# Scan groups of a two-block model on one core: order of the copies out of PSUM, of the z projections and of one convolution tap

## Chip, cores and metric

One core of a Trainium2 chip runs the whole program. The metric is the device time of one execution in microseconds (us), as the median of several runs. The engines are TensorE (PE in the rows, its weight loads PEld), VectorE (DVE), ScalarE (ACT), GpSimd (POOL) and SyncE (SP). Times inside the profile count from the start of the span.

## What is computed

The reference is one transformer block (stick-breaking and differential attention, gated FFN) and after it one hybrid block, everything in fp32. The change lies in the scan branch and the conformer branch of the second block, over 528 tokens (16 meta tokens and 512):

```
u = rms_norm(h, w_norm_mix);  proj = u @ w_in      # conf_a, conf_g, z, xbc, dt, gates
c = conf_a * sigmoid(conf_g)
c = depthwise_conv(c, 31 taps) ...                  # conformer branch
xbc = silu(depthwise_conv(xbc, 7 taps) + b)         # x (2048), B (4 x 128), C (4 x 128)
y = forward scan + backward scan of (x, dt, B, C) + d_skip * x
y = rms_norm(y * silu(z), w_ssm_norm)
merged = gates1 * (c @ w_conf_out) + gates2 * (y @ w_ssm_out)
h = h + merged @ w_out;  h = h + expert_choice_ffn(rms_norm(h))   # 16 experts
```

The scans are done in chunks of 128 tokens: within a chunk by a masked product of C and B with decays, between chunks by states.

## The kernel before

Each engine has its own program, a list in a fixed order, and the engines meet by semaphores. All activations lie in SBUF with channels on the 128 partitions and the 528 tokens along the free dimension. Projections of the second block (`dense`, line 499, called by `proj`, 774) are 32 matmuls each: 8 blocks of the contraction by two halves of 264 columns and two weight reads. A projection fills a pair of PSUM banks; the pairs 0-1 and 2-3 alternate, and `open_` waits until the pair's last content was freed. Banks 4 to 7 serve the scan. `fill` counts a bank as filled, `free` as freed, `got` and `freed` are the waits for these.

The four **scan groups** (`for g in range(GROUPS)`, in the program of each engine) have eight heads each, and each group runs through three stages.

**Conv stage.** Six projections `xbc(g, i, j)`, tiles t = 0 to 5 (four of x, one of B at t = 2, one of C at t = 5). ScalarE copies each from PSUM to `XP`, two buffers (`conv_tile`, line 1316). VectorE runs the seven taps into `CO`, two buffers (line 1870 for the first, 1873 for the other six), with two conformer taps between them. ScalarE applies silu (`conv_silu`, lines 1387 and 1389). TensorE turns the tile into token-major form by five transposes into banks 4 and 5 (`turn`, line 836), and ScalarE copies them out (`take_turned`, lines 1399 and 1400). TensorE's order is projection t, then transpose t-2. ScalarE's order for step t is tile copy t, silu t-1, copy of the turned tile t-3.

**z stage.** GpSimd scales the turned x by decay weights (`scaled`, line 2142), TensorE multiplies them with B into a state in bank 6 (line 866), VectorE folds it into the backward snapshots `SNAP` (lines 1885 to 1890) and then runs eight conformer taps (`some_taps(8, ...)`). There are four such state products per group, and behind each TensorE has one projection of z, on which ScalarE applies silu (line 1422). Ahead of the stage ScalarE issues four DMAs that fetch decay sums for two chunks, spread over all partitions (`fr_load`, line 1364), into two buffers `FR`; GpSimd masks them (`masked`, line 2153) and ScalarE makes exponentials of them (`decays`, line 1375).

**Chunk stage.** For each of five chunks (the last has 16 tokens) TensorE has one projection (a gate or, in groups 0 to 2, one half of a conformer pair, or the next group's first tile), the transpose of the last chunk's output (`turn_y`, line 845, bank 5), the products with the snapshots and the state (885, 890), eight small ones for the diagonal part (895), the next state (901) and the product of B and C for the next chunk (905). VectorE adds the two tables (1899), multiplies them by B·C (1903), combines the outputs (1915 to 1932), updates the state (1939 to 1944), and multiplies the turned output into z (`gate_y`, 1815). It runs two and two conformer taps in between. Table transfers for chunk c+2 wait until chunk c's tables were used. The last transpose of a group, `turn_y(g, NC-1)` at line 907, stands behind the fifth chunk, and VectorE's `gate_y(g, NC-1)` too.

**Conformer products.** For each of eight tiles u TensorE projects `ca` (a) and then `cg` (gate). ScalarE writes sigmoid of `cg` to `SGB` (`conf_gate`, line 1323), VectorE multiplies it with `ca` out of PSUM into `CP` (three buffers; `conf_in`, line 1844), and that frees the bank pair of `ca`. Tiles 0 and 1 are projected before the first group, the others in the chunk stages of groups 0 to 2. The 31 taps of each of the eight tiles, 248 in all (`conf_taps`, lines 1830 and 1833), are worked off in a fixed order `TAP_ORDER`; `some_taps` takes the next ones, but none of a tile that is not yet there.

Weights come through a ring of four slots, one load per SP instruction in a fixed order; a load waits for the last reader of its slot. Gates that fit nowhere later are projected at places listed in `GATES_AT` (in group 3 one more, "late", behind the conv stage), copied out by ScalarE and stored to HBM by a DMA of its queue (`gates_out`, line 1333).

Behind the scan groups come the layer norm and the output projections (from line 925), routing, and the expert stage (line 1047 and about it).

## Time and profile before

| | |
|---|---|
| runs | 2829.73 us median of 3 (2828.01 to 2834.2) |
| profiled execution | 2834.3 us, its span 2832.5 us |
| busy, share of the span | PE 94%, PEld 57%, DVE 36%, ACT 23%, POOL 8% |
| mean granted clock | 0.97 |
| chain that ended last | PE 88%, DVE 6%, ACT 2%, issue 2%, DMA 1%, POOL 1% |
| costliest lines | L1047 (experts) 509.8 and 504.8 us, L504 (projections) 545.1 us for 2304 matmuls |

How to read it: busy shares are of the whole span, which has stages with quite different limits. "Idle before, releaser" gives how long an engine stood before an instruction and what ended this. The granted clock is the share of full speed that TensorE had; it has two levels, 0.50 (1.2 GHz) and 1.00 (2.4 GHz). The first projection of the second block starts at 743.67 us, group 0 at 807.30, and the last instruction of group 3 ends at about 1460 us.

### The profile page before, as it was taken

Reading aid. Unit: us, or ns where it says so; the run is one execution under the profiler, and the core shown is the slowest. Engines: PE = TensorE matmul, PEld = TensorE weight load, DVE = VectorE, ACT = ScalarE, POOL = GpSimd, SP = SyncE. Lnnn points to the kernel's source line nnn. Section 1 sums busy time; section 2 is a strip of 40 time slices with the busy share of each in tenths; the row PEclk is TensorE's granted clock in tenths of the full one; section 3 lists DMA queues with packets and bytes.
Section 4 is the critical chain, followed back from the end, with each engine's and each line's share of the span. In section 5 each row is a group of like instructions: output and inputs, shape, how many; then the busy total and the mean of one; then the engine's idle time right before and its main releaser. Section 6 shows DMA issues by size and latency. Waiting matters only on the chain.

```text
span 2832.5 us, 39942 instructions
## 1 busy us (share of the span) xinstructions
PE 2657.5 (94%) x17315; PEld 1616.0 (57%) x17315; DVE 1028.0 (36%) x1482; ACT 654.7 (23%) x1166; POOL 214.1 (8%) x218
## 2 busy tenths in 40 slices
PE   8998999999979989898979997999999999999996
PEld 6754478888757767676767996333333333333332
DVE  4335344433246776676765434111111111111111
ACT  3245432222122314131226223000000000001001
POOL 0022000000002112030120000000000000000000
PEclk9999999999989999999989999999999999999998
DMA  5200032222214123230431244999999999999993
GB/s 198 88 2 1 30 119 90 89 82 86 105 43 130 55 71 103 71 103 23 118 117 60 90 172 161 403 391 402 400 393 402 395 407 398 395 402 392 392 399 142
DMA packets 92618, 560.77 MB, mean 198 GB/s; under 512 B 15236, under 2 KB 48004, under 8 KB 59812
## 3 DMA queue, kind: packets, MB, share of 16 engines
q1 hardware_dynamic: 40320, 514.89, 46.1%
q10 hardware_dynamic: 47236, 30.42, 4.0%
q0 software_dynamic: 4896, 12.98, 1.7%
q8 instruction: 137, 2.24, 0.3%
q14 instruction: 29, 0.24, 0.0%
HBM read 541.97 MB, written 16.29 MB: 197 GB/s over the span
## 4 chain that ended last, share of the span: by engine, by line
PE 88%; DVE 6%; ACT 2%; issue 2%; DMA 1%; POOL 1%; ACTq 0%; POOLq 0%; DVEq 0%
PE PS L1047 35%; PE PS L504 17%; PE PS L949 4%; PE PS L727 4%; PE PS L723 4%; PE PS L724 4%; PE PS L954 2%; PE PS L698 2%; PE PS L631 2%; PE PS L582 1%; PE PS L578 1%; PE PS L579 1%; PE PS L517 1%; PE PS L1037 1%; DVE H L1833 1%
## 5 line engine op out<-in xcount | busy, mean ns | idle before, releaser
L504 PE MATMUL PS<-U,ring 128*128 128x264 f32 x2304 | 545.1, 397 | 18.7 <-DVE arena L1844 18.7
L1047 PE MATMUL PS<-expert_ring_low,U 128*32 128x512 f32 x4608 | 509.8, 594 | 0.9 <-DVE U L2058 0.9
L504 PEld LDWEIGHTS PS<-U,ring 128*128 128x128 f32 x2304 | 448.8, 197 | 107.6 <-issue 29.5
L1047 PE MATMUL PS<-expert_ring_high,U 128*32 128x512 f32 x4608 | 504.8, 592 | 0.0
L1047 PEld LDWEIGHTS PS<-expert_ring_high,U 128*32 128x32 f32 x4608 | 148.0, 110 | 336.9 <-issue 335.9
L1047 PEld LDWEIGHTS PS<-expert_ring_low,U 128*32 128x32 f32 x4608 | 146.2, 110 | 332.9 <-issue 331.9
L1833 DVE SCALAR_TENSOR_TENSOR H<-arena,par,H 128x528 f32<-128x528 f32 x240 | 190.7, 840 | 1.4
L2070 DVE TENSOR_TENSOR H<-H,PS 128x512 f32<-128x512 f32 x32 | 22.0, 688 | 438.6 <-PE PS L1047 423.2
L723 PE MATMUL PS<-UX,WF 128*128 128x512 f32 x352 | 137.9, 392 | 0.8 <-DVE UX L1593 0.8
L724 PE MATMUL PS<-UX,WF 128*128 128x512 f32 x352 | 137.0, 389 | 0.0
L1270 ACT ACTIVATE WF<-ring 128x1024 fp32r<-128x1024 f32 (+1 forms) x76 | 72.0, 948 | 245.8 <-PE PS L727 245.5
L1539 ACT ACTIVATE H<-PS 128x512 f32<-128x512 f32 x32 | 19.1, 597 | 457.9 <-PE PS L1047 457.9
L1718 DVE TENSOR_TENSOR WF<-ring,WF 128x1024 fp32r<-128x1024 f32 (+1 forms) x76 | 82.5, 1085 | 93.3 <-ACT WF L1270 93.2
L1873 DVE SCALAR_TENSOR_TENSOR SQ<-arena,par,SQ 128x528 f32<-128x528 f32 x144 | 110.4, 767 | 3.4
L2200 POOL DMA_INDIRECT residual_rows<-H,scatter_rows x16 | 25.1, 1572 | 931.4 <-DVE H L2084 931.4
L1375 ACT ACTIVATE ring<-ring,arena 128x128 f32<-128x128 f32 (+1 forms) x320 | 89.2, 368 | 19.1 <-POOL ring L2153 16.8
L727 PE MATMUL PS<-UX,WF 128*128 128x512 f32 x352 | 87.0, 389 | 0.0
L2076 DVE COPY U<-PS 128x256 f32<-128x256 f32 x32 | 13.6, 425 | 191.1 <-PE PS L1041 191.1
L1550 ACT ACTIVATE SQ<-PS 2x512 f32<-2x512 f32 x32 | 18.9, 591 | 260.6 <-PE PS L1047 260.2
L1959 DVE TENSOR_TENSOR RINGL<-ring,WH 128x1024 fp32r<-128x1024 f32 x32 | 38.9, 1224 | 102.1 <-ACT WH L1461 102.1
L723 PEld LDWEIGHTS PS<-UX,WF 128*128 128x128 f32 x352 | 66.1, 188 | 15.3 <-DVE UX L1593 1.2
L724 PEld LDWEIGHTS PS<-UX,WF 128*128 128x128 f32 x352 | 66.1, 188 | 14.1 <-issue 0.5
(326 smaller groups left out, 3195.4 us busy)
## 6 DMA issues: line engine op xcount, KB each, us to landing
expert_ring_low<-w_experts SPq DMA_DIRECT2D x96, 2048.0 KB, 11.7
expert_ring_high<-w_experts SPq DMA_DIRECT2D x96, 2048.0 KB, 11.3
ring<-w_gu SPq DMA_DIRECT2D x11, 2048.0 KB, 7.8
ring<-ssd_sums ACTq DMA_DIRECT2D x32, 512.0 KB, 7.8
ring<-w_xbc SPq DMA_DIRECT2D x8, 1536.0 KB, 6.6
ring<-w_down SPq DMA_DIRECT2D x8, 1408.0 KB, 6.0
ring<-w_in SPq DMA_DIRECT2D x5, 2048.0 KB, 7.9
ring<-w_conf SPq DMA_DIRECT2D x8, 1024.0 KB, 5.4
```

The lines of the kernel that those rows point to most:

```text
L504: last = nc.tensor.matmul(PS[0:M, banks[i], 0:hi - lo], lhs(k), rhs(k)[:, lo:hi], start=(k == 0), stop=(k == K - 1))
L631: last = nc.tensor.matmul(PS[:, 3 + o // 512, o % 512:o % 512 + SEQ - k2 * P], lower if k2 == kb else ones, SP(h)[:, ZO[k2]:ZO[k2] + SEQ - ...
L723: nc.tensor.matmul(PS[:, bank, :], hi[:, k, :], src[:, 0, k0 + k, :], start=(start and k == 0), stop=False)
L724: nc.tensor.matmul(PS[:, bank, :], hi[:, k, :], src[:, 1, k0 + k, :], start=False, stop=False)
L727: last = nc.tensor.matmul(PS[:, bank, :], lo[:, k, :], src[:, 0, k0 + k, :], start=False, stop=(stop and k == n - 1))
L949: nc.tensor.matmul(PS[:, banks[i], 0:HT], wh[:, k, :], x(k)[:, lo:hi], start=(first and k == 0 and x is high), stop=False)
L1047: mm = nc.tensor.matmul(PS[QUAD * t:QUAD * t + QUAD, bank, :], stat(t), move(t), start=start, stop=stop)
L1270: A(split(0, p), raw(p), ACT.Copy).then_inc(S("fw_high"), 1)
L1375: ins = A(FR[i % 2][d][0:n, h, 0:n], FR[i % 2][d][0:n, h, 0:n], ACT.Exp, bias=FT[0:n, c, j:j + 1])
L1718: V_.tensor_tensor(split(1, p), raw(p), split(0, p).bitcast(F32), SUB).then_inc(S("fw_low"), 1)
L1833: ins = V_.scalar_tensor_tensor(acc, CP[:, u % 3, j:j + T2], par[:, w0 + j:w0 + j + 1], acc, MUL, ADD)
L1873: ins = V_.scalar_tensor_tensor(co, xp[:, k:k + T2], par[:, w0 + k:w0 + k + 1], co, MUL, ADD)
```

## The change

- `take_turned(g, t-3)` comes first in ScalarE's step t, ahead of the tile copy.
- A new `mid_tap` on ScalarE computes the middle one of the seven taps straight from PSUM into `CO`, as a Copy with a per-channel scale, and frees the bank pair; it waits until `CO` was read for tile i-2. VectorE does the other six taps, each adding to `CO`.
- `conf_gate` on ScalarE also copies `ca` from PSUM into `CP` and frees the pair; VectorE's `conf_in` multiplies it by `SGB` in place, counted by a new semaphore `conf_input`.
- Two z projections of a group go ahead of the state products: one ahead of transpose 4, one behind it. The other two follow state products 0 and 1. State product 3 follows the projection of chunk 0.
- `fr_load(g, 0)` and `fr_load(g, 1)` go ahead of `take_turned(g, 3)` on ScalarE.
- The last output transpose and product of a group go behind the next group's second projection and first conv tile.
- Four memsets of pads are chained instead of counted.

```diff
@@ TensorE
+            def z_gate(g, s):
+                name = ("z", g, s // 2)
+                arrived(name)
+                proj(("zt", 4 * g + s), slot(name), slice((s % 2) * P, (s % 2) * P + P), name)
+
+            def back_state(g, s):
+                c = NC - 1 - s
+                n = CHUNKS[c][1]
+                pe.wait_ge(S("xwb_ready"), 4 * g + s + 1)
+                open_(("sb", g, c), 6)
+                fill(nc.tensor.matmul(PS[:, 6, :], BT[0:n, c, :], XW[0:n, s % 2, :], start=True, stop=True), ("sb", g, c))
...
                     if t >= 2 or (g > 0 and t == 1):
                         xbc(g, i, j)
+                    if g > 0 and t == 1:
+                        turn_y(g - 1, NC - 1)
                     if t >= 2:
                         turn(g, t - 2)
                 gates((g, "conv"))
+                z_gate(g, 0)
                 turn(g, 4)
+                z_gate(g, 1)
                 gates((g, "late"))
...
-                for s, c in enumerate(range(NC - 1, 0, -1)):
-                    t0, n = CHUNKS[c]
-                    pe.wait_ge(S("xwb_ready"), 4 * g + s + 1)
-                    open_(("sb", g, c), 6)
-                    fill(nc.tensor.matmul(PS[:, 6, :], BT[0:n, c, :], XW[0:n, s % 2, :], start=True, stop=True),
-                         ("sb", g, c))
-                    name = ("z", g, s // 2)
-                    arrived(name)
-                    proj(("zt", 4 * g + s), slot(name), slice((s % 2) * P, (s % 2) * P + P), name)
+                for s in range(3):
+                    back_state(g, s)
+                    if s < 2:
+                        z_gate(g, s + 2)
                 for c, (t0, n) in enumerate(CHUNKS):
...
                     gates((g, c))
+                    if c == 0:
+                        back_state(g, 3)
...
-                turn_y(g, NC - 1)
+            turn_y(GROUPS - 1, NC - 1)
@@ ScalarE
                 b = bank(("xb", g, t))
-                free(A(tok(XP[:, i % 2, 3:3 + T2], T2), PS[:, b:b + 2, 0:HT], ACT.Copy), ("xb", g, t))
+                A(tok(XP[:, i % 2, 3:3 + T2], T2), PS[:, b:b + 2, 0:HT], ACT.Copy)
+
+            def mid_tap(g, t):
+                i = 6 * g + t
+                b = bank(("xb", g, t))
+                if i >= 2:
+                    g2, t2 = divmod(i - 2, 6)
+                    if t2 in (2, 5):
+                        act.wait_ge(S("conv_ready"), i - 1)
+                    else:
+                        got(act, ("tr", g2, t2))
+                w = pcol("ssm_w", conv_row(g, t) * SSM_TAPS + MID_TAP)
+                free(A(tok(CO[:, i % 2, :], T2), PS[:, b:b + 2, 0:HT], ACT.Copy, scale=w), ("xb", g, t))
 
             def conf_gate(u):
                 got(act, ("cg", u))
                 if u >= 1:
-                    act.wait_ge(*freed(("ca", u - 1)))
+                    act.wait_ge(S("conf_input"), u)
                 b = bank(("cg", u))
                 free(A(tok(SGB[:, :], T2), PS[:, b:b + 2, 0:HT], ACT.Sigmoid), ("cg", u))
+                if u >= 3:
+                    act.wait_ge(S("conf_tap"), TAPS_TO[u - 3])
+                b = bank(("ca", u))
+                free(A(tok(CP[:, u % 3, 15:15 + T2], T2), PS[:, b:b + 2, 0:HT], ACT.Copy), ("ca", u))
...
                 for t in range(6):
+                    if t >= 3:
+                        take_turned(g, t - 3)
                     if g > 0 or t >= 2:
                         conv_tile(g, t)
+                        mid_tap(g, t)
                     if t >= 1:
                         conv_silu(g, t - 1)
-                    if t >= 3:
-                        take_turned(g, t - 3)
+                fr_load(g, 0)
+                fr_load(g, 1)
                 take_turned(g, 3)
                 gates_out((g, "conv"))
                 conv_silu(g, 5)
+                take_gate(g, 0)
                 take_turned(g, 4)
+                take_gate(g, 1)
                 gates_out((g, "late"))
-                fr_load(g, 0)
-                fr_load(g, 1)
...
+                take_gate(g, 2)
+                take_gate(g, 3)
                 decays(g, 0)
                 decays(g, 1)
@@ VectorE
             def conf_in(u):
-                got(dve, ("ca", u))
-                dve.wait_ge(*freed(("cg", u)))
-                b = bank(("ca", u))
                 if u >= 3:
                     conf_taps(TAPS_TO[u - 3])
-                    dve.wait_ge(S("conf_tap"), TAPS_TO[u - 3])
-                free(V_.tensor_tensor(tok(CP[:, u % 3, 15:15 + T2], T2), tok(SGB[:, :], T2), PS[:, b:b + 2, 0:HT], MUL),
-                     ("ca", u))
+                dve.wait_ge(*freed(("ca", u)))
+                dve.wait_ge(*freed(("cg", u)))
+                cp = CP[:, u % 3, 15:15 + T2]
+                V_.tensor_tensor(cp, SGB[:, :], cp, MUL).then_inc(S("conf_input"), 1)
...
-                    for k in range(SSM_TAPS):
-                        if k == 0:
-                            ins = V_.tensor_scalar(co, xp[:, 0:T2], par[:, w0:w0 + 1], None, MUL)
...
+                    side_taps = [k for k in range(SSM_TAPS) if k != MID_TAP]
+                    for n, k in enumerate(side_taps):
+                        if n > 0:
+                            dve.wait_ge(S("conv_tap"), (len(side_taps) - 1) * i + n)
+                        V_.scalar_tensor_tensor(co, xp[:, k:k + T2], par[:, w0 + k:w0 + k + 1], co, MUL, ADD)\
+                            .then_inc(S("conv_tap" if n < len(side_taps) - 1 else "conv_done"), 1)
                         if k in (2, 5):
                             some_taps(1, 2 * g + 2)
+                    if g > 0 and t == 0:
+                        gate_y(g - 1, NC - 1)
...
-                gate_y(g, NC - 1)
+            gate_y(GROUPS - 1, NC - 1)
```

Not shown: the new helper `take_gate(g, s)` holds what stood in the loop over s (wait for projection s of z, silu into `YT`), `conv_row` and `MID_TAP` are names for what was written out, and `mid_tap(0, 0)` and `mid_tap(0, 1)` stand behind the first two tile copies. VectorE's wait for `CO` moved into `mid_tap`.

## Rows read from the trace of the kernel before

**Rows 1.** Stretch: us; length; busy (instructions) of PE, PEld, DVE, ACT, POOL; clock; DMA; GB/s
```profile
1800.00:2000.00 200.00, 200.00 (x1852) 64.15 (x1848) 22.71 (x43) 16.61 (x28) 11.79 (x9) 1.00 1.00 400
```

**Rows 2.** TensorE's waits over the run: for whom; us in total, times, longest
```profile
PE PS L836 <- ACT arena L1400: 29.5, 12, 5.3
PE PS L504 <- DVE arena L1844: 18.7, 8, 8.0
PE PS L845 <- DVE arena L1932: 10.7, 5, 2.5
PE PS L866 <- POOL arena L2142: 10.5, 3, 3.5
```

**Rows 3.** ScalarE in order of time, one tile of group 1: start, us, engine, line
```profile
1003.98 0.61 ACT L1316 ACTIVATE arena<-PS 128x528 f32<-128x528 f32 x1 [8.04 <-PE PS L504]
1004.49 0.73 ACT L1389 ACTIVATE SQ<-SQ,par 128x528 f32<-128x528 f32 x1
...
1005.74 0.27 ACT L1400 ACTIVATE arena<-PS 16x128 f32<-16x128 f32 x1
```

**Rows 4.** TensorE in order of time, with the idle time before each
```profile
788.58 17.12 PE L504 MATMUL PS<-U,ring 128*128 128x264 f32 x64 [8.00 <-DVE arena L1844]
...
827.65 1.30 PE L836 MATMUL PS<-consts_sb,SQ 128*128 128x128 f32 x5 [5.32 <-ACT arena L1400]
828.74 8.64 PE L504 MATMUL PS<-U,ring 128*128 128x264 f32 x32
...
968.19 0.57 PE L845 MATMUL PS<-consts_sb,arena 16*128 16x16 f32 x4 [2.42 <-DVE arena L1932]
...
1006.15 0.74 PE L836 MATMUL PS<-consts_sb,arena 128*128 128x128 f32 x5 [2.20 <-ACT arena L1400]
```

**Rows 5.** TensorE: two projections at full rate, one at the last slow place
```profile
897.29 14.41 PE L504 MATMUL PS<-U,ring 128*128 128x264 f32 x64
...
1325.99 8.97 PE L504 MATMUL PS<-U,ring 128*128 128x264 f32 x32
```

**Rows 6.** Stretches of TensorE alone: us; length; busy; clock; DMA; GB/s
```profile
963.00:968.00 5.00, 2.77 (x24) 1.00 0.00 0
968.00:974.00 6.00, 5.81 (x16) 0.50 0.00 0
```

**Rows 7.** VectorE: first and last instruction of one conv tile, group 1
```profile
986.90 0.49 DVE L1870 TENSOR_SCALAR SQ<-arena,par 128x528 f32<-128x528 f32 x1 [0.69 <-ACT arena L1316]
...
992.57 0.76 DVE L1873 SCALAR_TENSOR_TENSOR SQ<-arena,par,SQ 128x528 f32<-128x528 f32 x1
```

**Rows 8.** ScalarE's queue: the four table transfers of group 1
```profile
1026.46 6.77 ACTq L1364 DMA_DIRECT2D ring<-ssd_sums  x4
```

**Rows 9.** VectorE in group 3: last snapshot, eight taps, tables of chunk 0
```profile
1392.27 0.68 DVE L1887 TENSOR_TENSOR arena<-arena 128x512 f32<-128x512 f32 x1
...
1393.71 5.52 DVE L1833 SCALAR_TENSOR_TENSOR H<-arena,par,H 128x528 f32<-128x528 f32 x8
1401.83 1.23 DVE L1899 TENSOR_TENSOR ring<-ring 128x1024 f32<-128x1024 f32 x1 [2.60 <-ACT ring L1375]
```

**Rows 10.** TensorE in group 3, chunks 0 and 1
```profile
1402.24 1.02 PE L885 MATMUL PS<-arena 128*128 128x512 f32 x2
1404.37 2.00 PE L895 MATMUL PS<-arena 128*128 128x64 f32 x16 [1.11 <-DVE arena L1903]
...
1422.10 2.04 PE L901 MATMUL PS<-arena 128*128 128x512 f32 x2 [3.58 <-DVE arena L1917]
...
1424.36 7.80 PE L504 MATMUL PS<-U,ring 128*128 128x264 f32 x32
```

**Rows 11.** ScalarE's queue and GpSimd in group 3: tables of chunk 2
```profile
1407.37 1.47 ACTq L1364 DMA_DIRECT2D ring<-ssd_sums  x2
...
1416.77 2.62 POOL L2153 TENSOR_SCALAR_AFFINE_SELECT ring<-ring 128x1024 f32<-128x1024 f32 x2 [27.70 <-DMA ring<-ssd_sums]
1419.36 1.04 POOL L2142 TENSOR_TENSOR arena<-arena,par 128x512 f32<-128x512 f32 x1
```

More of the change, by code:

```diff
@@ L376, in slot, with conv_row @@
             return ring[:, slot_of[where[name]], at:at + k * n].rearrange("p (k n) -> p k n", k=k)
+        MID_TAP = SSM_TAPS // 2
+        def conv_row(g, t):
+            return 16 + (0 if t == 2 else 4) + g if t in (2, 5) else 4 * g + (t if t < 2 else t - 1)
         pieces = []
@@ L1337, in _ @@
             conv_tile(0, 0)
+            mid_tap(0, 0)
             conv_tile(0, 1)
+            mid_tap(0, 1)
             conf_gate(0)
@@ L1380, in conv_silu @@
                 act.wait_ge(S("conv_done"), i + 1)
-                j = 16 + (0 if t == 2 else 4) + g if t in (2, 5) else 4 * g + (t if t < 2 else t - 1)
+                j = conv_row(g, t)
                 co = CO[:, (6 * g + t) % 2, :]
@@ L1400, in take_turned, with take_gate @@
                 free(A(dst[0:META, 4, :], PS[0:META, 5, 0:P], ACT.Copy), tag)
+            def take_gate(g, s):
+                tag = ("zt", 4 * g + s)
+                got(act, tag)
+                b = bank(tag)
+                free(A(tok(YT[:, 4 * g + s, :], T2), PS[:, b:b + 2, 0:HT], ACT.Silu), tag)
             XS_AT = {0: 0, 1: 1, 3: 2, 4: 3}
@@ L1413, in _ @@
                 conv_silu(g, 5)
+                take_gate(g, 0)
                 take_turned(g, 4)
+                take_gate(g, 1)
                 gates_out((g, "late"))
-                fr_load(g, 0)
-                fr_load(g, 1)
-                for s in range(4):
-                    tag = ("zt", 4 * g + s)
-                    got(act, tag)
-                    b = bank(tag)
-                    free(A(tok(YT[:, 4 * g + s, :], T2), PS[:, b:b + 2, 0:HT], ACT.Silu), tag)
+                take_gate(g, 2)
+                take_gate(g, 3)
                 decays(g, 0)
@@ L1768, in _ @@
             for v in (XP[:, :, 0:3], XP[:, :, 3 + T2:6 + T2], CP[:, :, 0:15], CP[:, :, 15 + T2:30 + T2]):
-                V_.memset(v, 0.0).then_inc(S("pads"), 1)
+                link(V_.memset(v, 0.0))
             dve.wait_ge(S("dt_parts"), 2)
@@ L1801, in _ @@
             dve.wait_ge(S("w2_ready"), 1)
-            dve.wait_ge(S("pads"), 4)
             def bc(ap, n, w):
@@ L1828, in conf_taps @@
                     if j == 0:
-                        dve.wait_ge(*freed(("ca", u)))
+                        dve.wait_ge(S("conf_input"), u + 1)
                         ins = V_.tensor_scalar(acc, CP[:, u % 3, 0:T2], par[:, w0:w0 + 1], pcol("conf_b", u), MUL, ADD)
```

13 lines of the change are left out of this document (1 added, 12 removed).

## Prediction

> **What bounds the kernel now.** I read the stretches of the run first. TensorE is busy throughout the expert stage while the DMA engines run at their share of 1.00 [rows 1]; that stage starts when the layers before it end, so time taken out of the scan groups comes off the total one for one. Then the waits of TensorE over the whole run [rows 2]: the four longest lie in the scan groups or just ahead of them. They are the transposes (L836) behind ScalarE's copy of the transpose before (29.5 us in 12 waits), projections (L504) behind VectorE's conformer product (18.7 in 8), the last output transpose of a group (L845) behind VectorE (10.7 in 5), and the first state product (L866) behind GpSimd (10.5 in 3). Together that is 69.4 us. In time order one sees why: after a projection ScalarE does the tile copy, the silu and only then the copy of the turned tile [rows 3], while TensorE stands for 2.2 us, eleven times, and once for 5.3 us [rows 4].
>
> Idle time also costs clock. At full rate two projections take 14.41 us, 7.2 each; after idle or sparse stretches one takes 8.64 or 8.97 [rows 4, 5]. In the group transition the granted clock was 1.00 up to 968 us and 0.50, its 1.2 GHz level, for the six us behind it, after TensorE had stood for 2.4 us [rows 4, 6]. Nine such stretches after the start, the first at 828.74 and the last at 1325.99, lose 1.4 to 3.1 us each; with the small matmuls in front of them it is 19.8 us.
>
> **The change, part by part.** Every sum is against the profiled execution, 2834.3 us (span 2832.5 and 1.8 around it). That is 4.6 above the median of the runs, 2829.7, so I take what it saves off the median.
>
> Turned tiles copied first. ScalarE's copy of tile t-3 moves ahead of the wait for projection t. Its input is ready since the last projection, so the transpose t-2 finds its banks free. All 29.5 us go [rows 2]. Next late would be the silu for that transpose. In the steady state it has over 5 us: a VectorE tile takes 6.4 us today [rows 7] and 5.9 without its first operation, against a new tile period of 7.2+0.7, some 7.9 us. Only the very first transpose should wait, because VectorE starts that tile when the second conformer product is in: about 0.4 us new.
>
> Conformer products. ScalarE frees their banks itself, by two activations of 0.61 (as its tile copy) after the gate's projection. In the chunks the next user comes some 5 us later, so six waits of 1.5 us go, and the wait of 8.0 us ahead of the projections at 788.58 goes too, since the first product was ready long before VectorE finished its preamble [rows 4]. Only the wait of the first tile projection stays, 1.6 becoming 1.35. That is 17.4 us. The projections at 788.58 took 17.12 against 14.41; the clock was already half before the idle time, so I give that excess back nothing (bounds 0 and 2.7). VectorE's chunk loop is nearly as long as TensorE's, so about 0.15 us of wait returns in each of the six chunks: 0.9.
>
> z projections in front. Today the chain copy, GpSimd's scaling, state product leaves TensorE idle for 3.5 us in three groups. With one z projection ahead of the last transpose and one behind it, the chain (about 3 us) lies under 7.1 us of matmuls: 10.5 us go. The four table transfers move ahead too. They hold ScalarE's queue for 6.77 us [rows 8]. Behind them stand the copy of tile 3, the gate's copy and the last silu. All are wanted only after two projections, 15 us on, where the queue is free at about 11, so they cost nothing; without that cover it would be 4 x 6.8 us at most. SP's loads for z wait for slots that are released two stages earlier, and I find none late.
>
> Last output transpose behind the next group's second projection: three of the waits of 2.42 us go, 7.3 us; the fourth, after the last group, stays. VectorE multiplies it in after the next conv tile, 6 us ahead of the transpose that needs the bank.
>
> Middle tap. VectorE is rid of 0.49 us per tile [rows 7]. ScalarE gets 24 activations from PSUM; none like it is in the trace. The nearest rows are its plain tile copy, 0.61, and its silu with a per-channel operand, 0.73 [rows 3]. I take 0.73; either end is hidden, as VectorE has 2 us to spare in each tile. It waits for transpose t-2, which now follows the projection directly, and VectorE starts 1.5 us after the projection's end, sooner than behind today's transpose (2.9).
>
> New waits at the first chunk. The last state product now follows the first gate projection, so less stands between it and the first diagonal product (L895). VectorE must after it update the snapshot, run eight conformer taps, add the tables and multiply by them. In group 3 update and taps ran from 1392.27 to 1399.23, 6.96 us, and the rest from 1401.83 to the start of L895 at 1404.37, 2.54: 9.5 us without today's wait of 2.60 [rows 9, 10]. TensorE has a conformer projection and one product meanwhile, 8.0 us, in groups 0 to 2: with 0.1 us of signal 1.6 us idle, three times, 4.8. In group 3 there is no conformer projection, only the product at 1402.24 [rows 10], so 8.8 us idle, and after that a half-rate stretch worth up to 3.4 (2.7 by the excess at 788.58 and 0.7 for the small matmuls). It takes the place of today's 1.11 and 3.58 us and the 1.7 us by which the matmuls behind them are slow [rows 10]; the next tables, on which the 3.58 hung, are fetched meanwhile, as their buffer comes free with those products: 12.2 less 6.4 is 5.8 us lost.
>
> The sum: removed idle 29.5+17.4+10.5+7.3 = 64.7; clock given back 19.8; new 0.4+0.9+4.8+5.8 = 11.9. Net 72.6, so 2834.3 becomes 2761.7 and the median 2757.1, **2757 us**.
>
> On the clock, the Trainium skill, TensorE: Matmul & The Clock Gate, section What's actually happening, says that the throttled state is the default and that the activity monitor runs free of the kernel, so the same work can lose the clock in one place and not in another. The trace agrees: of eleven equal waits of 2.20 us only one, ahead of 1325.99, is followed by a slow projection [rows 5]. By that rule some of the 19.8 may be lost elsewhere; that is the first rival.
>
> **The rivals.**
> First, the clock does not come back: the new gaps of 1.6 us and the sparse end of each group still drop it as often. For it: not only the longest gaps preceded the falls. Against: in the chunks with such gaps the clock mostly held, and the long ones vanish. All 19.8 lost again: 2777.
>
> Second, the start of the chunks costs nothing, because the taps in the last state slot end sooner or are used up: 4.8 and 5.8 us fall away, 2746. Against it: the order of taps gives eight in that slot in every group.
>
> Third, the tables come late. The transfer for chunk 2 is issued when the first products are done, now 9.6 us after the last state product. In group 3 GpSimd started on such a transfer 9.4 us after its issue and worked 3.6 us before VectorE could go on [rows 11]. In my walk it is just in time in groups 0 to 2, by 0.3 us. With 2 to 3 us lost in each group it is 9 more: 2766.
>
> Fourth, the middle tap closes a loop through ScalarE and VectorE: copy 0.61, tap 0.73, taps 5.9, silu 0.73, copy of the turned tile 0.9 and transpose 0.7 in series are 9.6 us per tile against 7.9, over 22 tiles 38 us: 2795. It ends **slower** than before only if the tap takes over 2.6 us, since 22 times another 1.9 us are needed. Against it: two buffers part consecutive tiles, and its nearest rows take 0.61 and 0.73.
> The Trainium skill, ScalarE: Activation LUTs, section Rules for kernel authors, advises VectorE and not ScalarE for a multiplication, and so speaks against this part. The rows agree on the direction (0.61 against 0.49 for one pass) [rows 3, 7], and I raise this rival's chance for it.
>
> Fifth, the change does not do what it says: the transposes turn out to wait for the silu, whatever the copies do. Then 29.5 us and some clock stay: 2789. Against it: today the copy ends 0.14 us before the transpose starts (1006.01 and 1006.15) [rows 3, 4], and the silu of the tile concerned ran a whole period earlier.
>
> **How the numbers follow.** Forecast 0.62, first 0.15, second 0.08, third 0.10, fourth 0.03 (0.02 of it slower), fifth 0.02. A measurement of this kernel tells about 0.2% (5.7 us) from no change. Faster 0.97, same 0.01, slower 0.02. The range goes down past the second rival by the start's clock (2.7) and up past the first: 2744 to 2779.
>
> **What would show it.** Right: no L836 wait on L1400's successor beyond 1 us; no L866 wait on GpSimd; one L845 wait of 2.4 left; projections of 7.28 in the conv and z stages; a new wait of L895's successor on VectorE, 1.5 us in groups 0 to 2 and near 9 us in group 3; the tap at 0.6 to 0.75. Wrong: TensorE waiting for silu or middle tap at each tile, GpSimd's table masking ending the waits in the chunks, or half-rate stretches where nothing idles.

## The result, and the profile after it

The changed kernel takes **2757.9 us** (median of 4 runs, 2756.73 to 2761.74), the kernel before beside it 2829.69 (2828.01 to 2834.2). The ratio is 0.9746, with a 95% interval of 0.9729 to 0.9763. The forecast was 2757 in a range of 2744 to 2779. The profiled execution of the new kernel is the slowest of its four, 2761.74 with a span of 2760.0; that of the kernel before was 2834.3 with a span of 2832.5. The two profiles are 72.5 us apart.

The first place to look is what TensorE still waits for over the whole run. The view gives the waiting line, the engine and line that released it, us in total, the number of waits, and the longest.

```profile
PE PS L915 <- DVE arena L1940: 11.3, 4, 6.8
...
PE PS L921 <- DVE arena L1954: 4.1, 9, 1.7
...
PE PS L850 <- DVE arena L1969: 3.3, 2, 2.4
```

Against [rows 2]: the transposes (now L841) and the state products (L865) have no row left, the projections (L509, in the next rows) have 1.3 us instead of 18.7, and of the output transposes (L850) two waits stand where five did, the 2.4 us one at the very end and one of 0.9 that was there before too. New at the top is the first diagonal product of a group (L915), which waits for VectorE's tables; 11.3 us in four waits. (The row of L921, 4.1 us in nine short waits, is the successor of L901, which had 5.7 us before.) All rows of this view together gave 152.5 us before and 97.2 now.

The page of the profile has the other half of the gain, in its first part and in the row of the projections (us busy, mean ns of one, idle time before it):

```profile
PE 2640.1 (96%) x17315; PEld 1608.2 (58%) x17315; DVE 1012.5 (37%) x1458; ACT 673.3 (24%) x1198; POOL 215.7 (8%) x218
...
L509 PE MATMUL PS<-U,ring 128*128 128x264 f32 x2304 | 527.4, 389 | 1.3 <-ACT arena L1360 1.3
```

TensorE executes the same 17315 matmuls and was busy for 2657.5 us before. So 55.3 us came from waits and 17.4 from matmuls that ran at a better clock; 72.7 in all, against 72.5 between the two spans. The granted clock over the run went from 0.970 to 0.976.

Where in the run that lies is seen by cutting both executions at the first projection of the second block and at the end of the last output transpose (stretch; length; busy and matmuls of TensorE; clock; DMA; GB/s). Before, then after:

```profile
743.67:1459.49 715.82, 636.19 (x2905) 0.95 0.27 80
742.83:1387.03 644.20, 619.28 (x2905) 0.98 0.29 89
```

The stage became 71.6 us shorter with the same 2905 matmuls. What follows it, the expert stage included, took 1373.0 us before and 1373.0 after, so its time did come off the total one for one, as the forecast had assumed.

In order of time, TensorE at the start of the groups, and then the first chunks of groups 0, 1 and 3 (start, us, engine, line, and in brackets the idle time before it):

```profile
779.67 16.05 PE L509 MATMUL PS<-U,ring 128*128 128x264 f32 x64
797.02 7.36 PE L509 MATMUL PS<-U,ring 128*128 128x264 f32 x32 [1.30 <-ACT arena L1360]
804.21 0.71 PE L841 MATMUL PS<-consts_sb,SQ 128*128 128x128 f32 x5
804.76 7.29 PE L509 MATMUL PS<-U,ring 128*128 128x264 f32 x32
...
884.70 2.00 PE L915 MATMUL PS<-arena 128*128 128x64 f32 x16 [1.48 <-DVE arena L1940]
886.54 1.08 PE L921 MATMUL PS<-arena 128*128 128x512 f32 x2
...
1030.24 2.09 PE L915 MATMUL PS<-arena 128*128 128x64 f32 x16 [1.48 <-DVE arena L1940]
1032.12 2.02 PE L921 MATMUL PS<-arena 128*128 128x512 f32 x2
...
1323.99 1.12 PE L905 MATMUL PS<-arena 128*128 128x512 f32 x2 [1.51 <-DVE arena L1927]
1331.94 3.68 PE L915 MATMUL PS<-arena 128*128 128x64 f32 x16 [6.82 <-DVE arena L1940]
1335.41 2.02 PE L921 MATMUL PS<-arena 128*128 128x512 f32 x2
1337.22 0.63 PE L925 MATMUL PS<-arena 128*128 128x128 f32 x2
1337.65 8.06 PE L509 MATMUL PS<-U,ring 128*128 128x264 f32 x32
```

A tile of the convolution stage is now a projection of 7.29 us and transposes of 0.71 with nothing between them; where [rows 4] had 2.20 us of idle time, there is none. The 8.00 us ahead of the first projections are gone too. The new waits stand where the forecast put them: 1.48 us in groups 0, 1 and 2, and in group 3 1.51 and 6.82, 8.33 together, with matmuls at half rate behind them. The stretches of TensorE there (us; length; busy and matmuls; granted clock; DMA; GB/s) show the lower of its two levels, 1.2 GHz, after TensorE had stood for 6.82 us, and then its return:

```profile
1332.00:1338.00 6.00, 6.00 (x21) 0.50 0.64 124
1338.00:1345.00 7.00, 7.00 (x30) 0.91 0.21 46
```

On VectorE's side of group 3 what ends the long wait is this chain of snapshot, eight taps and tables:

```profile
1323.25 0.69 DVE L1927 TENSOR_TENSOR arena<-arena,PS 128x512 f32<-128x512 f32 x1
1323.97 5.52 DVE L1878 SCALAR_TENSOR_TENSOR H<-arena,par,H 128x528 f32<-128x528 f32 x8
1329.41 1.21 DVE L1936 TENSOR_TENSOR ring<-ring 128x1024 f32<-128x1024 f32 x1
1330.66 1.22 DVE L1940 TENSOR_TENSOR arena<-ring,PS 128x1024 f32<-128x1024 f32 x1
```

ScalarE's middle tap, which no row of the kernel before could price directly, takes 0.70 us right behind the tile copy; the tile here is one of group 2:

```profile
1097.16 0.61 ACT L1336 ACTIVATE arena<-PS 128x528 f32<-128x528 f32 x1 [4.42 <-PE PS L509]
1097.71 0.70 ACT L1349 ACTIVATE SQ<-PS,par 128x528 f32<-128x528 f32 x1
```

### The profile page after: what moved, and what is told of

It reads as the page before. It is cut to its first block, busy times and chain, and to the rows that moved or that the text cites. A ratio compares the mean times of both kernels' runs of the same rounds, so it can differ in the third digit from the quotient of the medians.

```text
span 2760.0 us, 39931 instructions
## 1 busy us (share of the span) xinstructions
PE 2640.1 (96%) x17315; PEld 1608.2 (58%) x17315; DVE 1012.5 (37%) x1458; ACT 673.3 (24%) x1198; POOL 215.7 (8%) x218
## 4 chain that ended last, share of the span: by engine, by line
PE 90%; DVE 7%; issue 1%; ACT 1%; DMA 0%; POOL 0%; POOLq 0%; ACTq 0%; DVEq 0%; SPq 0%
PE PS L1067 36%; PE PS L509 17%; PE PS L969 5%; PE PS L732 4%; PE PS L728 4%; PE PS L729 4%; PE PS L974 2%; PE PS L703 2%; PE PS L636 2%; DVE H L1878 1%; PE PS L583 1%; PE PS L584 1%; PE PS L587 1%; PE PS L522 1%; PE PS L1057 1%
## 5 line engine op out<-in xcount | busy, mean ns | idle before, releaser
L509 PE MATMUL PS<-U,ring 128*128 128x264 f32 x2304 | 527.4, 389 | 1.3 <-ACT arena L1360 1.3
L509 PEld LDWEIGHTS PS<-U,ring 128*128 128x128 f32 x2304 | 436.7, 191 | 80.6 <-issue 8.5
L1414 ACT ACTIVATE ring<-ring,arena 128x128 f32<-128x128 f32 (+1 forms) x320 | 89.3, 369 | 17.4 <-POOL ring L2190 14.4
## 6 DMA issues: line engine op xcount, KB each, us to landing
expert_ring_low<-w_experts SPq DMA_DIRECT2D x96, 2048.0 KB, 11.3
```

Of the source, the lines that this page charges most:

```text
L509: last = nc.tensor.matmul(PS[0:M, banks[i], 0:hi - lo], lhs(k), rhs(k)[:, lo:hi], start=(k == 0), stop=(k == K - 1))
L1414: ins = A(FR[i % 2][d][0:n, h, 0:n], FR[i % 2][d][0:n, h, 0:n], ACT.Exp, bias=FT[0:n, c, j:j + 1])
```

## The experiments

My theory was the one of the forecast: each part takes a wait of TensorE away, the waits stand in series, and the first chunk gets a new one. The rivals were that parts overlap (one wait hides another, so that a part alone is worth little), that the middle tap matters in one direction or the other, and that something else than VectorE's order of taps sets the new wait. Twelve kernels were run, each timed in several rounds beside the kernel before. All times are medians of four runs. The kernel before had 2833.49, 2832.37 and 2833.55 us in the three sessions of these runs, and 2829.69 beside the new kernel. Where a run is compared with the new kernel below, the difference in us is that of the medians; by the ratios to the kernel before it comes out up to 3 us differently, and the intervals are those of the ratios.

**The middle tap back on VectorE** (a1_tap_back). The new kernel without that part; VectorE's seven taps are again as in the kernel before (not shown).

```diff
-                A(tok(XP[:, i % 2, 3:3 + T2], T2), PS[:, b:b + 2, 0:HT], ACT.Copy)
+                free(A(tok(XP[:, i % 2, 3:3 + T2], T2), PS[:, b:b + 2, 0:HT], ACT.Copy), ("xb", g, t))
...
-                        mid_tap(g, t)
```

> The changed kernel with the middle tap back on VectorE (seven taps there, the tile copy alone frees the banks). Theory: the tap was hidden on both engines, since a tile takes VectorE 6.4 us against a tile period of 7.7 to 7.9; 2757 us, within 3 of the changed kernel, and TensorE's waits stay as they are. Rival (relief of VectorE pays): 24 tiles x 0.49 us come back, up to 2770.

Measured: 2758.94 us, ratio 0.9746 [0.9728, 0.9764], the same ratio as with the tap on ScalarE. The longest row of waits is unchanged:

```profile
PE PS L915 <- DVE arena L1944: 11.3, 4, 6.8
```

Moving the tap moves no time that these runs could tell from nothing.

**The tap done four times** (c3_tap_again). The tap's activation is issued three more times (`EXTRA` is 3), with the same result.

```diff
+                for _ in range(EXTRA):
+                    link(A(tok(CO[:, i % 2, :], T2), PS[:, b:b + 2, 0:HT], ACT.Copy, scale=w))
```

> The changed kernel with ScalarE's middle tap done four times over, so that each tile holds the banks and VectorE's start back by 2.2 us more. Theory (the tap is hidden): ScalarE's work per tile is 5.1 us and VectorE's 5.9, both under 7.7; within 4 us of the changed kernel, 2757 to 2762. Rival (ScalarE and VectorE work in series per tile): 22 tiles x 2.2 us, 48 us, over 2800.

Measured: 2760.19 us, 0.9746 [0.9729, 0.9762]. ScalarE's tile of group 2, in order of time, has the additional work in it:

```profile
1101.55 2.17 ACT L1351 ACTIVATE SQ<-PS,par 128x528 f32<-128x528 f32 x3
1103.75 0.70 ACT L1352 ACTIVATE SQ<-PS,par 128x528 f32<-128x528 f32 x1
```

VectorE starts two tiles of that stage, in the same kernel, at these times:

```profile
1096.82 2.38 DVE L1911 SCALAR_TENSOR_TENSOR SQ<-arena,par,SQ 128x528 f32<-128x528 f32 x3 [1.75 <-ACT SQ L1352]
...
1104.48 2.38 DVE L1911 SCALAR_TENSOR_TENSOR SQ<-arena,par,SQ 128x528 f32<-128x528 f32 x3 [1.77 <-ACT SQ L1352]
```

The tap now takes 2.87 us instead of 0.70, yet the tiles follow each other in 7.66 us, TensorE's own period (7.29 and 0.71, less their overlap), and VectorE still waits 1.75 us in each. The two buffers let the tile of VectorE slide behind by 2.2 us without lengthening the period. So the fourth rival's closed loop does not exist at this length: above a tap of 2.6 us it had the kernel slower than before, and at 2.87 us it is as fast as with 0.70. Runs with a longer tap were not made.

**The turned copy late again** (a2_copy_late). On top of a1: the copy of the turned tile stands behind the tile copy and the silu. It has to be on top of a1, since with the tap on ScalarE the old order would close a circle: the tap of tile t waits for transpose t-2, that transpose for the copy of tile t-3, and this copy would stand behind the tap in ScalarE's own order. This is read off the program and was not run. By it the early copy is a precondition of the tap on ScalarE.

```diff
-                    if t >= 3:
-                        take_turned(g, t - 3)
                     if g > 0 or t >= 2:
                         conv_tile(g, t)
                     if t >= 1:
                         conv_silu(g, t - 1)
+                    if t >= 3:
+                        take_turned(g, t - 3)
```

> As the one before, and the turned tile's copy again behind the next tile's copy and silu. Theory: the twelve waits of the transposes return, eleven of 2.2 us and one of about 5 (29.5 us), with 2 to 5 us of half-rate stretches: 2787 to 2792. Rival (the silu, not the copy, released the transposes): no difference to the kernel before it in the list. Rival (clock is the larger part): more than 40 us, over 2797.

Measured: 2796.49 us, 0.9875 [0.9858, 0.9892]; 37.5 us more than a1. TensorE's waits and its order of time in group 0:

```profile
PE PS L841 <- ACT arena L1437: 29.8, 12, 5.7
```

```profile
818.33 1.30 PE L841 MATMUL PS<-consts_sb,SQ 128*128 128x128 f32 x5 [5.67 <-ACT arena L1437]
819.42 9.53 PE L509 MATMUL PS<-U,ring 128*128 128x264 f32 x32
831.15 0.74 PE L841 MATMUL PS<-consts_sb,arena 128*128 128x128 f32 x5 [2.20 <-ACT arena L1437]
831.72 7.29 PE L509 MATMUL PS<-U,ring 128*128 128x264 f32 x32
841.21 1.30 PE L841 MATMUL PS<-consts_sb,SQ 128*128 128x128 f32 x5 [2.20 <-ACT arena L1437]
842.30 15.47 PE L509 MATMUL PS<-U,ring 128*128 128x264 f32 x64
```

The row of twelve waits is back, in the same place and of nearly the same size as in [rows 2]; the fifth rival (the transposes wait for the silu) is refuted. I had expected 2787 to 2792 and missed: the waits cost 28.8 us as thought (all waits 95.5 in a1, 124.3 here), but TensorE's busy time grew by another 8.3 us (2638.9 to 2647.2). That is still less than the waits, so that run's second rival (clock the larger part) does not hold either, though the total came out just below the 2797 that it was given. The rows show 4.4 of the 8.3 us: the wait of 5.67 is followed by a projection of 9.53 us instead of 7.29, and of two waits of 2.20 us one is followed by a projection of 7.29, the other by transposes of 1.30 instead of 0.71 and two projections of 15.47 instead of 14.41. The rest lies mostly at one such place in each of groups 1 and 2.

**The early copy alone** (d1_copy_early). The same edit the other way round, in the kernel before.

> The kernel before with one part of the change alone: ScalarE's copy of a turned tile stands first in its step of a tile, ahead of that tile's projection copy and silu. Theory (each part keeps its worth when it stands alone): the 12 waits of TensorE's transposes for ScalarE's copies (29.5 us in the kernel before) are gone, and with them the clock that they cost. The run that took this part back out of the new kernel lost 28.8 us of idle and 8.3 us of clock, so this one gains 34 to 38 us on the kernel before (about 2832): 2794 to 2798, ratio 0.987. Rival (the parts overlap: the 8 waits for the conformer product and the other waits of the old order take up slack that this part frees): under 29 us of gain, 2803 or more, with some other row of TensorE's waits grown. My step in the forecast priced this part at 29.5 us of idle and the share of the 19.8 us of clock that falls to its waits.

Measured: 2798.19 us, 0.9877 [0.9857, 0.9897]; 35.4 us less than the kernel before. The waits for turned tiles are gone and the next three rows are as they were:

```profile
PE PS L504 <- DVE arena L1844: 18.7, 8, 8.0
PE PS L845 <- DVE arena L1932: 10.7, 5, 2.5
PE PS L866 <- POOL arena L2142: 10.5, 3, 3.5
```

All waits together are 30.2 us less, the busy time 4.6. The part is worth about as much alone (35.4 us) as when it is taken out last (37.5), so within the few us that the runs resolve it overlaps with none of the others.

**The conformer product**, taken back out of the new kernel (a3_product_back) and put alone into the old one (d2_product_split). Of the first:

```diff
-                    act.wait_ge(S("conf_input"), u)
+                    act.wait_ge(*freed(("ca", u - 1)))
...
-                free(A(tok(CP[:, u % 3, 15:15 + T2], T2), PS[:, b:b + 2, 0:HT], ACT.Copy), ("ca", u))
...
+                free(V_.tensor_tensor(tok(CP[:, u % 3, 15:15 + T2], T2), tok(SGB[:, :], T2), PS[:, b:b + 2, 0:HT], MUL),
+                     ("ca", u))
```

> The changed kernel with the conformer product again taken by VectorE from PSUM, freeing the banks. Theory: the wait of 8.0 us in front of group 0 returns and six waits of 1.5 us in the chunks, less some 1 us of waits that vanish: 16 to 19 us, 2773 to 2776. Rival (the chunk loop is bound by VectorE anyway): only the 8.0 us, 2766.

> The kernel before with the conformer product's part of the change alone: ScalarE copies the projection out of PSUM behind its sigmoid, and VectorE multiplies in SBUF. Theory: the 8 waits of the projections for VectorE's product (18.7 us in the kernel before) shrink to one of about 1.3 us, as in the new kernel; 17.4 us of idle, and 1 to 5 us of clock, since the part's removal from the new kernel cost 21 us: 2811 to 2815, ratio 0.993 to 0.994. Rival (ScalarE's copy, in a kernel where ScalarE still copies turned tiles late, stands in the way of a silu or a turned tile's copy): the wait for turned tiles grows from 29.5 us and the gain stays under 14 us, 2819 or more.

Measured: without the part 2779.06 us, 0.9814 [0.9798, 0.9831], 21 us more than the new kernel; the part alone 2811.17 us, 0.9926 [0.9903, 0.9949], 22.4 us less than the kernel before. With the part taken out, TensorE's wait is the old one to the digit:

```profile
PE PS L509 <- DVE arena L1885: 18.7, 8, 8.0
```

In the waits it is 17.0 us one way and 18.1 the other, as forecast (17.4). TensorE's busy time changed by 1.4 us in the first pair of profiles and by 7.0 in the second, so how much clock comes with the part is not settled. The part alone came out inside its expectation (2811 to 2815); the part taken out, expected at 2773 to 2776, missed it by 3 us. The rival of d2, that ScalarE's copy would lengthen the waits for turned tiles, did not happen: 29.9 us in twelve.

**The z projections, table transfers and last state product in their old places** (a4_z_back). Not shown are the removal of `back_state(g, 3)` behind the first gate and ScalarE's order of copies and transfers, which follows.

```diff
-                z_gate(g, 0)
                 turn(g, 4)
-                z_gate(g, 1)
...
-                for s in range(3):
+                for s in range(4):
                     back_state(g, s)
-                    if s < 2:
-                        z_gate(g, s + 2)
+                    z_gate(g, s)
```

> The changed kernel with the four z projections again each behind a state product, the four table transfers again behind the last turned tile, and no state product behind the first gate. Theory: three waits of 3.5 us and their half-rate stretches return (10.5 and 8), but the waits for VectorE at the start of the chunks, 1.5 us three times and 8.3 us with slow matmuls in group 3, go (about 10 to 13 net of the 4.7 us that group 3 had): 2761 to 2768. Rival (the reordering was worth its whole 18.5 us): 2775.

Measured: 2761.65 us, 0.9754 [0.9738, 0.977]. Only 3.7 us more than the new kernel by the medians and 0.7 by the two profiled executions; the intervals overlap widely. The waits show an exchange, and TensorE in group 1 has slow matmuls behind the returned one:

```profile
PE PS L865 <- POOL arena L2174: 10.5, 3, 3.5
...
PE PS L916 <- DVE arena L1949: 6.4, 9, 3.6
```

```profile
988.87 2.04 PE L865 MATMUL PS<-arena 16*128 16x512 f32 x2 [3.48 <-POOL arena L2174]
990.84 9.51 PE L509 MATMUL PS<-U,ring 128*128 128x264 f32 x32
```

The 10.5 us for GpSimd's scaling return, and of the 11.3 us at the first diagonal product only the 1.11 us of the kernel before are left. The clock is exchanged too: behind the three returned waits the projections take 9.07, 9.51 and 9.41 us instead of 7.28, but no slow matmuls stand behind the first diagonal product any more, and the busy time is the same (2639.5 us against 2640.1). So this part of the change took one wait and made another of the same size. The run undoes three moves at once; whether the z projections in front, with the last state product left in its old place, would have kept the gain without the new wait was not run. This is the part with something left in it, which the next experiments look for.

**The last output transpose at the end of its group** (a5_last_transpose_back), and VectorE's `gate_y` with it (not shown).

```diff
-                    if g > 0 and t == 1:
-                        turn_y(g - 1, NC - 1)
...
-            turn_y(GROUPS - 1, NC - 1)
+                turn_y(g, NC - 1)
```

> The new kernel with one part undone: the last chunk's output transpose of groups 0 to 2, and VectorE's gating behind it, stand again at the end of their group and not behind the next group's second projection. Theory: 7.3 us of idle come back at the transpose in four parts of about 2 us (three of them in groups 0 to 2, and the wait at the end stays), and up to 4 us of clock behind them; 2765 to 2769, ratio 0.9772 to 0.9786. Rival (the wait is covered by something that runs late anyhow, or moving it only shifts a wait into the next group's first transpose): within 2 us of the new kernel, 2756 to 2760.

Measured: 2769.7 us, 0.9782 [0.9764, 0.98]; 11.8 us more. The wait is back, at 7.2 us more than in the new kernel:

```profile
PE PS L850 <- DVE arena L1965: 10.5, 5, 2.4
```

The remaining 4 to 5 us can't be seen in this profile: its execution was the fastest of the four (2764.0, the others 2769.23 to 2770.53) and had a granted clock of 0.978 against 0.975 and 0.976. They are the clock of the other three executions, as far as the numbers go; which matmuls lost it is open.

**The conformer taps moved out of the last state slot** (b1_taps_earlier). If VectorE's eight taps between the last state product and the tables set the new wait, then six of them must go elsewhere. A tile of the convolution stage has room for one more: in the new kernel VectorE waits 1.75 us for the middle tap in a tile of group 2, as it does in the tiles of c3 shown above.

```diff
-                        if k in (2, 5):
+                        if k in (1, 2, 5):
...
-                    some_taps(8, 2 * g + 2)
+                    some_taps(8 if s < 3 else 2, 2 * g + 2)
```

> The changed kernel with three conformer taps in each conv tile instead of two, and two instead of eight behind the last state product: the same 44 taps per group ahead of the chunks. Theory: VectorE reaches the first diagonal product 4.1 us sooner after the last state product (9.5 becomes 5.4), under the 8.0 us that TensorE has in groups 0 to 2, so three waits of 1.5 us go; in group 3 the wait of 6.8 becomes 2.7; the half-rate matmuls behind these waits (3 to 5 us) go too: 11 to 14 us less, 2744 to 2747. A conv tile takes VectorE 6.6 us, still under 7.7, so no transpose waits. Rival (those waits only move: the tables of chunk 2 or VectorE in the chunks release TensorE instead): under 4 us, 2754 or more.

Measured: **2744.13 us**, 0.9688 [0.9672, 0.9704], 13.8 us less than the new kernel. Waits fell from 97.2 to 86.6 us and busy time from 2640.1 to 2631.8. In groups 0 to 2 the wait at the first diagonal product is gone and in group 3 it is 2.75 instead of 6.82:

```profile
1317.86 3.68 PE L915 MATMUL PS<-arena 128*128 128x64 f32 x16 [2.75 <-DVE arena L1940]
```

The second rival of the forecast was nearly built here: a first chunk without its wait, except in group 3, gives 2744, where it had said 2746 for all four.

**The late gate of group 3 behind the third state product** (b2_late_gate_moved), so that TensorE has 7.3 us of work where it stood. ScalarE's copy of it moves behind the first decays (not shown, like the condition that keeps the old place of the state product in groups 0 to 2).

```diff
-                gates((g, "late"))
...
+                    if c == 0 and g == GROUPS - 1:
+                        gates((g, "late"))
+                        back_state(g, 3)
                     gates((g, c))
```

> The changed kernel with the late gate projection of group 3 between its third and its last state product. Theory: of group 3's two waits of 1.5 and 6.8 us about 1.5 stays, as in the other groups, and its slow matmuls (about 4 us) become quick: 9 to 11 us less, 2747 to 2749. Rival (group 3 is bound by the table transfers): the wait turns up behind GpSimd in chunks 1 and 2, and under 4 us are won, 2754 or more.

Measured: 2748.74 us, 0.9702 [0.9685, 0.9718]. All four waits at the first diagonal product are now the short one:

```profile
1326.34 2.00 PE L917 MATMUL PS<-arena 128*128 128x64 f32 x16 [1.48 <-DVE arena L1942]
```

**Both** (b3_both).

> Both of the edits before. Theory: no wait of the first diagonal product in any group; 12.7 us of idle time and 5 to 7 us of half-rate time less than the changed kernel: 2738 to 2741. Rival: they overlap in group 3 only by 4 us, so the sum of both less 4 to 7; anything above 2745 means that a wait has moved.

Measured: 2741.83 us, 0.9675 [0.9659, 0.9691]; only 2.3 us less than b1 alone, whose interval it overlaps, and just outside what I had expected (2738 to 2741). The waits at the first diagonal product are gone in all groups, but another has come up in the profile of b3. TensorE in group 3, chunk 1:

```profile
1332.82 1.54 PE L923 MATMUL PS<-arena 128*128 128x512 f32 x2 [2.81 <-DVE arena L1956]
```

VectorE, GpSimd and ScalarE with its queue (ACTq), of the same kernel, back from that wait:

```profile
1331.15 0.69 DVE L1954 TENSOR_TENSOR arena<-PS,arena 128x512 f32<-128x512 f32 x1 [0.94 <-POOL arena L2181]
...
1327.05 2.60 POOL L2192 TENSOR_SCALAR_AFFINE_SELECT ring<-ring 128x1024 f32<-128x1024 f32 x2 [17.27 <-DMA ring<-ssd_sums]
...
1315.31 0.61 ACT L1372 ACTIVATE arena<-PS 128x528 f32<-128x528 f32 x1 [2.11 <-PE PS L509]
...
1316.32 1.85 ACTq L1405 DMA_DIRECT2D ring<-ssd_sums  x2
```

The table transfer for chunk 2 was issued at 1316.32, behind the copy of a gate for which ScalarE had stood 2.11 us; its buffer was free since VectorE's last reading of it, which ended about 1313.5. GpSimd masked the table when it had landed and only then did its other work, for which VectorE and TensorE waited. This is the forecast's third rival, the tables that come late; it appears only once the wait in front of it is gone.

**The transfer ahead of the gate copy** (b4_load_first), on top of b3.

```diff
+                    if c == 0:
+                        fr_load(g, 2)
                     gates_out((g, c))
...
-                    if c + 2 < NC:
+                    if 0 < c < NC - 2:
                         fr_load(g, c + 2)
```

> The best version so far (three conformer taps in each tile of the convolution, two instead of eight in the last state slot, and group 3's late gate between the third and fourth state products; 2741.8) with one more edit: ScalarE issues the table transfer of chunk 2 ahead of the loop's first gate copy and not behind it. There the transfer of group 3 was issued 2.8 us after its buffer was free, and TensorE then waited 2.81 us for the table of chunk 1, or what stands with it, through VectorE, GpSimd's masking and that transfer. Theory (the gate copy in front of the transfer is that wait): the 2.8 us are gone or down to 1 us, 2738 to 2740.5. Rival (the wait comes from the transfer's own length, or VectorE's order, and moves on): within 1 us of 2741.8. Second rival: ScalarE's wait for the freed buffer now holds back the gate copy, TensorE's next gate product waits for its PSUM bank: 2743 to 2746.

Measured: **2738.11 us**, 0.9668 [0.965, 0.9686]. ScalarE's queue, GpSimd and TensorE of this kernel:

```profile
1313.82 1.03 ACTq L1405 DMA_DIRECT2D ring<-ssd_sums  x2
...
1324.35 2.14 POOL L2194 TENSOR_SCALAR_AFFINE_SELECT ring<-ring 128x1024 f32<-128x1024 f32 x2 [14.25 <-DMA ring<-ssd_sums]
...
1331.35 1.10 PE L923 MATMUL PS<-arena 128*128 128x512 f32 x2 [1.02 <-DVE arena L1958]
```

The transfer is issued 2.5 us earlier, GpSimd masks 2.7 us earlier, TensorE's wait is 1.02 us and the product behind it runs at full rate. That 1.8 of the wait's 2.81 us hung on the gate copy is shown. That the total fell with it is not, as the intervals of b3 and b4 overlap. Against the kernel before, b4 is the fastest of all versions, 3.3% below it, and about 20 us below the new kernel.

## Why the prediction was right, by its steps

**Turned tiles, 29.5 us: right.** 28.8 us of waits came back when the part was undone in the new kernel, and 30.2 went when it was put alone into the old one. The 0.4 us foreseen for the very first transpose did not come: there is no wait at L841.

**Conformer product, 17.4: right,** with 17.0 and 18.1. Its wait at the first tile projection is 1.30, as I had it 1.35. At the start I gave nothing back of the excess of 2.7 us; the projections took 16.05 instead of 17.12, so 1.1 came back, inside the bounds.

**z projections and table transfers, 10.5: right in the wait, and little in the net.** The forecast's terms nearly said so, had I drawn the sum for this part: 10.5 removed, against 4.8 and 4.1 of new idle time (8.8 less 1.11 and 3.58). They also gave it about 6.5 us of clock behind the three old waits (projections of 10.39, 9.07 and 8.89 us instead of 7.28), against 1.7 lost in group 3, so some 6 us would have been left. What they missed is the 3.6 us of clock behind the new waits of groups 1 and 2, which leaves about 3. a4 measures 0.7 us by the profiles and 3.7 by the medians.

**Last output transpose, 7.3: right,** 7.2 by a5.

**Middle tap at nothing: right,** and its duration 0.70 against the 0.73 that I took. The fourth rival is refuted by c3; the step in it that fails is that it puts the operations of one tile in series, while the two buffers let tiles overlap. The Trainium skill, ScalarE: Activation LUTs, section Rules for kernel authors, would have had the multiplication on VectorE. The rows agree that one pass is shorter there, 0.49 against 0.70 us, though the first reads from SBUF and the second from PSUM; the two runs with and without it show that here neither choice costs time.

**New waits at the first chunk: right.** 1.48 three times where I had 1.6. In group 3 8.33 of idle time where I had 8.8; it did not stand at the diagonal product alone, as my sign had it, but with 1.51 of it at the product with the snapshot (L905). Behind it came 3.8 us of excess at half rate (3.68 us against 1.89, 2.02 against 1.02, 0.63 against 0.38, and 8.06 against 7.29) where I had 3.4. Of the 0.9 us for the chunk loop nothing appears at the projections: L509 has a single wait, the first.

**Clock.** The sum of the gain in the rows is 55.3 of waits (forecast 54.5: 64.7 less 10.2) and 17.4 of busy time (forecast 18.1: 19.8, less 3.4, plus 1.7). That was the least safe term, and that it came out so near is in part luck: behind the waits of 1.48 us in groups 1 and 2 the clock does fall (the product takes 2.02 us instead of 1.08, and 3.6 us are lost in the two stretches together), which I had not counted; 1.1 came back at the start, which I had not counted either, and about 2 more that were not traced to a place. As four executions of the new kernel differ by 5 us, a part of that may be no effect of the change. The first rival, that the clock would be lost elsewhere, is thereby right in kind and wrong in size: 3.6 us of its 19.8. The Trainium skill, TensorE: Matmul & The Clock Gate, section What's actually happening, has the activity monitor run free of the kernel; the rows agree in so far as equal waits have unequal ends, with the same 1.48 us followed by full rate in group 0 and by half rate in group 1, and the same 2.20 us in a2 likewise.

**Additive.** By their medians the parts are worth 35.4 (early copy), 22.4 (conformer product), 11.8 (last transpose), 3.7 (z) and about 1 (tap), 74 in all, against 71.8 for the whole; by the ratios they are some 68. In TensorE's waits alone, which repeat better, they are 30.2, 18.1, 5.8, 1.3 and -1.7 us, 53.7 in all, against 55.3. A large overlap between the parts is thereby excluded; an interplay of a few us is not. On an engine that is otherwise busy through the whole stage, as TensorE is here, the waits in series did add up.

## What to carry to other kernels

When one engine bounds a stretch, list its waits, and order each helper engine's queue by who is waiting: a copy that frees a PSUM bank goes ahead of work that no one needs for another 5 us. Here that order alone gave 35 us. Count a moved step twice, for the wait that it removes and for the work that it no longer shields, since the z projections' 10.5 us were paid back in full by waits of 11.3 at the next place. Then shorten that next wait by moving work to where the same engine has proven slack: six conformer taps per group, moved from in front of the tables into the tiles, gave 14 us, more than the z part of the change.

## What the runs showed of the hardware beyond that

The clock behind a wait costs a surcharge that is not the same each time. The same twelve waits cost 28.8 us idle and 8.3 busy when put into the new kernel, and taking them out of the old one gave 30.2 and 4.6. Executions of one kernel differ too: the kernel before ran in 2825.86 to 2834.38 us in one session, with a granted clock of 0.974 in the shortest run and of 0.970 in the longest; the version a5 in 2764.0 to 2770.53. A single profile can therefore hide or add some 5 us of a part's worth, which is more than the difference between 8.3 and 4.6; whether the surcharge depends on the kernel around the waits is not shown. Waits far from the edits moved less from profile to profile: that for GpSimd in the first block (L631 in the kernel before) is 8.0 us in three waits in all fourteen, and the one of 9.3 us for VectorE behind the scan groups (L1014 there) lies between 8.2 and 9.3.
